# Differential attention on one core: stationary rows split once and reloaded, two sets of keys and values, ascending tiles

## What is computed

```
q, k, v = split(h @ w_in);  q, k = rms_norm(q), rms_norm(k)      # per head: q, k (2, 64), v (128)
p = softmax(where(mask, q k^T * scale, -inf))                    # for each of the two maps m
pd = p[0] - lam * p[1]
o = rms_norm(pd @ v) * (1 - lambda_init);  y = o @ w_out
```

## Time and profile before

| what | us |
|---|---|
| median of three runs | 3237.12 |
| span of the profiled execution (its first to its last instruction) | 3232.7 |
| rows and projections of head 0 | 0 to 133 |
| attention | 133 to 1604 |
| output projection, residual, second norm | 1604 to 1830 |
| MLP | 1830 to 3233 |
| TensorE busy | 2982.7 (92%) |
| VectorE, ScalarE, GpSimd busy | 1740.7, 1420.1, 1114.5 |

### The profile page before, as it was taken

One profiled execution on the slowest core, in us unless ns is written; L12 is line 12 of the kernel. 1 busy time (PEld: TensorE's weight loads), 2 busy tenths in 40 slices (PEclk: granted clock), 3 DMA queues, 4 the chain that ended last, 5 costly groups with the idle time before them and its releaser, 6 DMA issues. The chain is left out here.

```text
span 3232.7 us, 47903 instructions
## 1 busy us (share of the span) xinstructions
PE 2982.7 (92%) x15680; PEld 2552.7 (79%) x15680; DVE 1740.7 (54%) x3093; ACT 1420.1 (44%) x3531; POOL 1114.5 (34%) x1228
## 2 busy tenths in 40 slices
PE   7798998989899898987599899999999999999999
PEld 6687887878788787876488688888888888888887
DVE  6687887878788887877533222322222222222223
ACT  5577776767677676766422211222222221111111
POOL 6545454554545455540300122222222212222221
PEclk9899999999999999989699899999999999999999
DMA  3100000000000000010134511111112511111111
GB/s 107 45 5 21 13 17 17 17 17 6 28 6 18 16 17 17 6 60 7 53 118 169 189 40 52 52 52 52 52 52 103 209 40 49 42 39 51 40 52 71
DMA packets 149207, 163.06 MB, mean 50 GB/s; under 512 B 8464, under 2 KB 114960, under 8 KB 149008
## 3 DMA queue, kind: packets, MB, share of 16 engines
q1 hardware_dynamic: 142512, 135.43, 13.1%
q10 hardware_dynamic: 6496, 25.17, 2.0%
HBM read 127.01 MB, written 33.55 MB: 50 GB/s over the span
## 5 line engine op out<-in xcount | busy, mean ns | idle before, releaser
L1441 PE MATMUL banks<-u,w_hi 128*128 128x512 f32 x2048 | 632.1, 390 | 10.4 <-POOL w_lo L1326 10.4
L1336 POOL TENSOR_TENSOR hid_lo<-relu_sq,hid_hi 128x512 fp32r<-128x512 f32 x128 | 165.9, 1296 | 1022.4 <-ACT hid_hi L1387 1022.4
L1384 ACT ACTIVATE relu<-banks 128x512 f32<-128x512 f32 x128 | 76.6, 598 | 956.3 <-PE banks L1441 956.3
L1441 PEld LDWEIGHTS banks<-u,w_hi 128*128 128x128 f32 x2048 | 385.4, 188 | 90.9 <-POOL w_lo L1326 10.8
L1424 DVE TENSOR_TENSOR y<-banks,y 128x512 f32<-128x512 f32 x256 | 176.9, 691 | 460.6 <-PE banks L1458 460.6
L629 ACT ACTIVATE p_all<-scores,bias 128x512 f32<-128x512 f32 (+3 forms) x640 | 392.8, 623 | 50.6 <-DVE bias L615 47.6
L1441 PE MATMUL banks<-u,w_lo 128*128 128x512 f32 x1024 | 399.1, 390 | 0.0
L1458 PE MATMUL banks<-w_hi,hid_hi 128*128 128x512 f32 x1024 | 398.3, 389 | 0.0
L1458 PE MATMUL banks<-w_lo,hid_hi 128*128 128x512 f32 x1024 | 398.3, 389 | 0.0
L1458 PE MATMUL banks<-w_hi,hid_lo 128*128 128x512 f32 x1024 | 398.3, 389 | 0.0
L608 DVE TENSOR_REDUCE mx<-scores 128x1 f32<-128x512 f32 (+3 forms) x640 | 365.1, 602 | 50.0 <-PE scores L599 48.0
(11 more groups left out here) (111 smaller groups left out, 5661.1 us busy)
## 6 DMA issues: line engine op xcount, KB each, us to landing
w_raw<-in_mlp_w SPq DMA_DIRECT2D x128, 512.0 KB, 4.1
w_raw<-in_a_w_in SPq DMA_DIRECT2D x96, 128.0 KB, 2.3
p_all<-in_x SPq DMA_DIRECT2D x16, 512.0 KB, 3.5
rows_scratch<-o_sum SPq DMA_DIRECT2D x128, 64.0 KB, 1.6
o_in<-rows_scratch SPq DMA_DIRECT2D x16, 512.0 KB, 4.5
x_res<-in_x SPq DMA_DIRECT2D x16, 512.0 KB, 5.3
rows_scratch<-h_out SPq DMA_DIRECT2D x16, 512.0 KB, 3.0
y<-rows_scratch ACTq DMA_DIRECT2D x2, 4096.0 KB, 15.3
```

The costliest lines, as they stand in the source:

```text
L1441: last = pe.matmul(banks[:, e, :], w[:, j % 2, kt, :], u[:, n * TPB:(n + 1) * TPB, kt, :], start=(kt == 0 and w is w1_hi and u is u_hi), s ...
```

## The change

The attention is written anew, with the same products and the same sums up to their order. A step is now numbered a = 16 h + j, and j is the tile.

- Rows: each turned tile is split once, in the first block, into a ring of four slots in SBUF (`u_ring`, 1 MB each), ScalarE the high part, VectorE the low. Both parts are stored to DRAM (`u_dram`) and loaded again for each of the heads 1 to 7 by `load_u`, 112 loads of 1 MB on the SyncE queue. The splits L260 and L266 and `u_keep` are gone.
- Keys and values have two sets (`k_s`, `v_s`), used by even and odd heads; keys hold high and low in one tile, queries are in `q_hi` and `q_lo`. The matmuls are as many as before.
- Tiles go from the first to the last.
- Maxima and exponentials take pieces of up to two banks (1024 columns); with one piece the maximum gives the bias itself. The combine is one instruction over the whole row, ahead of the first maximum of the step, and transposes of p wait for all of it.
- The q/k norm is always on GpSimd. The constant eps is a 65th column of the squares, so an addition goes. In the first block the low half of v moves from VectorE to GpSimd.
- The two blocks are one, the loop over heads is written out, and the weights of head h + 2 are split in the step j = 15.

The core of the diff:

```diff
-            pe.wait_ge(u_lo_set, 2 * n + half + 1)
+            if hp == 0:
+                pe.wait_ge(u_lo_set, n + 1)
+            else:
+                pe.wait_ge(u_loaded[n % US], 16 * ((n - NT) // US + 1))
...
+        def dve_max(dve, a, m):
+            t, par, np = a % NT, a % 2, pieces_of(a % NT)
+            for k in range(np):
+                width = piece_width(t, k)
+                dve.wait_ge(scored, score_count(a, m, min(2 * k + 1, banks_of(t) - 1)))
+                piece = flat[:, k * 2 * BANK:k * 2 * BANK + width]
+                if np == 1:
+                    dve.tensor_reduce(bias[:, par, m:m + 1], piece, AX.X, ALU.max, negate=True)\
+                       .then_inc(bias_set, 1)
+                else:
+                    dve.tensor_reduce(mx[:, m, k:k + 1], piece, AX.X, ALU.max).then_inc(piece_max, 1)
...
+        def load_u(sp, n):
+            sp.wait_ge(proj_half, 2 * (n - US) + 2)
+            if n - NT < US:
+                sp.wait_ge(u_stored[n % US], 16 * (NT // US))
+            sp.dma_start(u_ring[:, n % US].rearrange("p a k r -> p (a k r)").bitcast(F32), u_dram[n % NT])\
+              .then_inc(u_loaded[n % US], 16)
...
+                for j in range(2, NT):
+                    sp.wait_ge(u_normed, j - 1)
+                    sp.dma_start(x_in[:, j % 2, :], x[j * P:(j + 1) * P, :]).then_inc(x_loaded[j % 2], 16)
+                    store_u(j - 2)
+                load_weights(sp, 1, (0, 1))
+                store_u(NT - 2)
+                store_u(NT - 1)
+                for n in range(NT, NT + 3):
+                    load_u(sp, n)
+                load_weights(sp, 1, (2, 3))
...
+                    for k in range(np):
+                        act_exp(act, a, 0, k)
+                    if a and n - 1 < ALL and late:
+                        act_turned_qk(act, n - 1)
+                    if a:
+                        act_turned_p(act, a - 1, 0)
+                    if a and n - 1 < ALL:
+                        act_v(act, n - 1)
+                    if a >= 2:
+                        act_square_output(act, a - 2)
+                    if n < ALL:
+                        act_keep_qkv(act, n)
+                        act_square_qk(act, n)
+                    if j == NT - 1 and h + 2 < H:
+                        act_split_weights(act, h + 2, (0, 1))
+                    if a and nb > 1:
+                        act_turned_p(act, a - 1, 1)
+                    if a >= 2:
+                        act_norm_output(act, a - 2)
+                    act_exp(act, a, 1, 0)
+                    if a and nb > 2:
+                        act_turned_p(act, a - 1, 2)
+                    if np > 1:
+                        act_exp(act, a, 1, 1)
+                    if j == NT - 1 and h + 2 < H:
+                        act_split_weights(act, h + 2, (2, 3))
+                    if a and nb > 3:
+                        act_turned_p(act, a - 1, 3)
...
+                    if a:
+                        dve_combine(dve, a - 1)
+                    dve_max(dve, a, 0)
+                    if a and n - 1 < ALL:
+                        dve_turned_qk(dve, n - 1)
+                    if a >= 2:
+                        dve_output(dve, a - 2)
+                    if a:
+                        dve_turned_p(dve, a - 1, 0)
+                    if j == NT - 1 and h + 2 < H:
+                        low_weights(dve, h + 2, 1)
+                    if n < ALL and j < 8:
+                        dve_sum_qk(dve, n)
+                    dve_max(dve, a, 1)
+                    if a and nb > 1:
+                        dve_turned_p(dve, a - 1, 1)
+                    if n < ALL and j >= 8:
+                        dve_sum_qk(dve, n)
+                    if a and nb > 2:
+                        dve_turned_p(dve, a - 1, 2)
+                    if j == NT - 1 and h + 2 < H:
+                        low_weights(dve, h + 2, 3)
+                    if a and nb > 3:
+                        dve_turned_p(dve, a - 1, 3)
...
+                    pe_scores(pe, a, 0)
+                    if a >= 2:
+                        pe_values(pe, a - 2, banks_of((a - 2) % NT) - 1)
+                    if a and n - 1 < ALL and j >= 8:
+                        pe_turn_qk(pe, n - 1)
+                    if a == 0:
+                        pe_project(pe, n, 0)
+                    if n < ALL:
+                        pe_project(pe, n, 1)
+                    if a and n - 1 < ALL and j < 8:
+                        pe_turn_qk(pe, n - 1)
+                    if a:
+                        pe_turn_p(pe, a - 1, 0)
+                    pe_scores(pe, a, 1)
+                    if a and nb > 1:
+                        pe_turn_p(pe, a - 1, 1)
+                        pe_values(pe, a - 1, 0)
+                    if n + 1 < ALL:
+                        pe_project(pe, n + 1, 0)
+                    if a:
+                        for g in range(2, nb):
+                            pe_turn_p(pe, a - 1, g)
+                            pe_values(pe, a - 1, g - 1)
```

959 lines of the change are left out of this document (398 added, 561 removed).

## The result

The changed kernel takes 3324.97 us (median of 4 runs, 3324.16 to 3325.33), the kernel before 3237.05 beside it: a ratio of 1.027, 95% interval 1.0255 to 1.0284. It is slower by 88 us. Forecast were 14 us slower and a range up to 3305. The direction came out, the size did not.

The account below looks back on a forecast made before the run. TensorE was taken to bound attention (831.08 of 925 us busy), with 31 us of waits a head. Terms 130.6 + 8.9 + 146.15 + 6 x 190.75 + 178.4 gave 1608.6 for 1604, with clock allowance 1618 (+14): 3251 us, range 3167 to 3305.

Parts of the forecast that it names:

- the steps of 3 and 4 tiles: Small attention steps: 9.05 and 9.3 us, together 18.35 for 16.0 before.
- the step of 16 tiles: Largest step of a head, next weights split inside it, low piece ahead of the second maximum: 19.5 us instead of 15.7.
- the last head with its drain: Last head, no projection: 178 us from the end of head 6's fifteenth tile, 15 of it draining four groups.
- Steps of 5 to 8 tiles: Attention steps with the second maximum behind one thread to the sum: 9.95, 10.5, 10.3, 10.65 us, together 41.4 for 37.2.
- Steps of 9 to 15 tiles: Larger attention steps, ending with the p group behind the projection: 9.6, 11.1, 11.6, 12.3, 13.05, 13.55, 15.2 us.
- TensorE loses its clock: Rival: idle gaps at the change of head keep 1.2 GHz through small steps, 50 us in all, 3300; 8 in 100.
- The allowance of 9 us: Added to the sum: 1.5 us per change of head for a lower clock while TensorE idles there.
- The two steps at the change of head: Steps of 1 and 2 tiles, behind the weight splits and the old tile's values: 25.1 us for 31.0.
- Head 0's rows: First block: 6.1 us a tile for 6.85, 11 us less, the last qkv at 114.7.
- Start of attention: ScalarE waits for head 1's weights behind three 1 MB loads: first step ends 16 us after the last qkv, at 130.6.
- the reload: Rows loaded again in heads 1 to 7: 1 MB a step, 3.8 us, hidden by steps of 9 us or more.
- chains hidden: Rival: small and middle steps cost as before, 178.8 us a head, 84 less in all, 3167 to 3180; chance 0.34.

Follow-up runs that it names:

- best version: The change with qkv copy and output earlier, next weights split apart, large steps' first maximum before the combine, output-weight split after it, GpSimd, load and low-piece reorders: 3180.55 us.
- the last run: The best version with the coefficient's z, in steps of up to 8 tiles, made by a sum over one element instead of a copy: 3179.20 us.

## Why the prediction was right or wrong

The direction was right for its own reason in part: chains in order cost more than the engines' relief brings. The size was wrong by three terms above all: the steps of 3 and 4 tiles, where the sum had no wait of TensorE for the copy of qkv, the step of 16 tiles, where TensorE's wait for the weights' low piece was missing, and the last head with its drain.

One reading of the rows was off by a tile, and it hides where a head loses. Tiles fall before the change, so the 55.9 us of the earlier trace rows are the steps of 15 to 12 tiles and not of 16 to 13, and so on down. Size by size, in us, as the mean of heads 1 to 6 (counted from 0), from the distances between coefficients:

| steps of | before | forecast | change | best version |
|---|---|---|---|---|
| 1 and 2 tiles | 17.6 | 25.1 | 24.3 | 22.2 |
| 3 and 4 | 17.1 | 18.35 | 21.6 | 17.2 |
| 5 to 8 | 39.5 | 41.4 | 42.0 | 38.3 |
| 9 to 12 | 47.9 | 44.6 | 45.4 | 44.0 |
| 13 to 15 | 42.8 | 41.8 | 41.9 | 40.1 |
| 16 | 20.2 | 19.5 | 21.6 | 15.7 |
| a head | 185.0 | 190.75 | 196.7 | 177.4 |

Steps of 9 tiles and more but the largest are cheaper after the change. What it loses lies in the small steps, about half of it in those of 1 and 2 tiles, which the forecast had nearly right. No run takes that part away: the best version keeps 4.6 of the 6.7 us. (The last of the six heads has no weights to split, so its step of 16 tiles is short and lowers the mean.) By its steps:

- *Steps of 5 to 8 tiles*: forecast 9.95, 10.5, 10.3, 10.65; measured, mean of heads 1 to 6, 10.4, 10.65, 10.1, 10.8. The thread over q and k, output, square, copy, sum is there link by link: the second maximum starts right behind the sum. For 5 and 6 tiles some luck is in it: the step of 5 tiles takes 9.8 us in some heads and 11.0 in others, that of 6 tiles 11.3 or 10.3, by where the clock falls, and the forecast meets their mean.
- *Steps of 9 to 15 tiles*: forecast 9.6, 11.1, 11.6, 12.3, 13.05, 13.55, 15.2; measured 9.7, 11.6, 11.7, 12.4, 13.2, 14.0, 14.7. Right, and the last head has nearly the same lengths with no projection (14.4 and 14.5 for 14 and 15 tiles).
- *Steps of 3 and 4 tiles*: forecast 9.05 and 9.3, measured 10.9 and 10.65. **This step failed in kind.** The sum followed the scores' thread, and let TensorE project whenever it was its turn. It left out that a half projection of the next tile now stands one scores step behind the end of this one, and that the copy between them stands behind the output's square on ScalarE. TensorE waits 2.3 to 2.7 us there, 2.0 in the step of 5 tiles. The prediction said what a moved instruction is queued behind on VectorE, and not who waits for the copy. Before the change the two halves of one tile were a step's halves, and the copy had the rest of the step. Moving the copy, and then the output, took 64 us away in all step sizes together.
- *The clock*: the rival "TensorE loses its clock" was given 8 in 100 with the change of head as its cause. The clock did fall, in three to five half projections a head, behind the waits for the copy and for the weights and at the start of the next head; the granted clock of 300 to 1500 us is 0.96, above the 0.93 set as its threshold, and the time came out beyond its 3300. The allowance of 9 us in my sum left the small steps out.
- *Step of 16 tiles*: forecast 19.5, measured 23.1 (15.1 in head 6, where no weights are split, for 15.7 forecast). What the weights add was sized at 3.8 us and is 8.0. The sum had the low piece ahead of the second maximum and missed the other queue: TensorE's half projection waits for the same piece, with two groups of transposes behind it. Moving the piece changed nothing; splitting the weights a step earlier brought some 6 us a head over the two steps.
- *The two steps at the change of head*: forecast 25.1, measured 23.5 in four heads, 25.1 and 26.4 in two.
- So a head was 198 where 190.75 was forecast: some 44 us over six heads, 20 of them in the steps of 16 tiles, 19 in those of 3 and 4, 9 in those of 5 to 15, less 5 in those of 1 and 2.
- *Head 0's rows*: forecast 6.1 us a tile and 114.7 for the last qkv, measured 6.2 and 6.65 in turn and 122.2, 7.5 us more. The interval lay between two bounds, a DMA time and TensorE's need, and no wait names either as the bound; the waits lead over ScalarE, VectorE and GpSimd. The first interval, 10.6 us, was not in the sum.
- *Start of attention*: first coefficient 21.2 us after the last qkv, 16 forecast; the wait for the weights is there (ScalarE waits until 133.3), and the loads of rows ahead are not its cause.
- *Last head*: from the coefficient of head 6's fifteenth tile (1488.8) to the end of attention at about 1690 (as much ahead of the next matmul, 1691.7, as the 1604 of before is ahead of 1605.4) some 201 us, 178 forecast. The drain was put at 15 and is about 22 (last coefficient 1668.1): a combine of 4.3 us, which GpSimd's subtraction nearly doubled, and four groups, partly at half the clock. The step of 16 tiles ahead of it is 18.0, where 15.7 was forecast, with the same doubling in it. The other 14 us lie in steps that my sum gave only as one number, which is why they can't be laid to a term.
- *Costed at nothing and right*: the reload. No load of rows ends any wait of a projection in 300 to 1500 us; it takes 5.1 us from issue to landing, where 3.8 was forecast.

The tally: 14 forecast, 13 ahead of attention, 2 in head 0, 44 in six heads, 23 in the last, 4 in the output projection, less the 9 of the clock allowance: 91, by which the two profiled spans differ (3323.4 and 3232.7); the medians differ by 88.

The rival "chains hidden" (0.34) took the order of instructions as harmless. It was beaten by the order, and the experiments show how near it was: with no work added or taken away, other orders of the changed kernel's instructions, loads and waits run from 3180 to 3498 us. The best version's heads take 177 to 178.5 us, near the 178.8 of this rival, but by another path: its steps of 1 and 2 tiles and of 16 are shorter than the rival's sum has them, and those of 5 to 8 longer than the 37.2 it took over.

## What to carry to other kernels

For each instruction that moves, ask two questions: what is it now queued behind, and which engine waits for its result with what in its own queue. A sum along the path of the scores answers the first and misses the second, and for an engine at 90% a wait of 2 to 3 us can cost twice, in time and in clock afterwards. When an engine is relieved and the time does not fall, list the waits of the fullest engine by releaser; two lines of such a list, the copy and the weights, led to 43 and 34.5 us here, and both were cured by order alone. Compare the whole list after each move, too: in three runs the wait that was attacked went or shrank, and another engine's result took its place.

## What the runs showed of the hardware

- A gap of 2.0 to 2.7 us on TensorE, waiting for the copy, was followed by most of the clock's loss, but not each time. In heads 1 to 6 of the changed kernel there are 24 such gaps. Behind 15 the matmuls of 384 columns start 0.32 us apart in place of 0.17 to 0.18, and the twelve of a half projection take 3.3 to 3.6 us from first to last start; behind the other nine they take 2.0. The gap of 2.26 us in the step of 4 tiles is of both kinds, three times each. So such a gap costs another 1.3 to 1.6 us behind it, or nothing. With the copy moved the gaps in the steps of 2 to 4 tiles are 1.0 to 1.2 us, and none was followed by a half projection at the lower clock. What decides in between isn't shown.
- VectorE's combine and GpSimd's subtraction exclude each other by who starts first, by as little as 0.04 us (1650.42 against 1650.46): the loser's row shows its own time and the rest of the winner's. The Trainium skill (SBUF — State Buffer, section "SBUF: two separate sides") says that the one that starts first holds the pair of ports for its whole instruction; the trace agrees in both directions.
- Even a copy of two elements pays that. In small steps z, VectorE and GpSimd of the changed kernel:

```profile
566.55 0.79 DVE L425 COPY z<-z_part 128x2 f32<-128x2 f32 x1 [0.84 <-ACT p_all L414]
...
566.28 1.04 POOL L288 TENSOR_TENSOR qk_nat<-qkv,qk_rs 128x512 f32<-128x512 f32 x1
```

The copy ends when GpSimd's instruction does. The power on four elements that GpSimd does just before (L284) holds no copy: copies that start beside it take 0.17 us. A sum over the same elements, and the reciprocal and the product behind it, are not held: in the last run they start with up to 0.96, 0.99 and 0.86 us of the same instruction of GpSimd to go, and take 0.16, 0.17 and 0.28 at most.
